# Two cache loads written as eight separate runs per partition, with unpadded source arrays

## The reference

```python
xn = rmsnorm(x, norm1)
z  = xn @ w_in                         # one projection, split into ten parts
a_o, state = hgrn2_scan(...)           # group A: gated linear recurrence, 4 heads of 128
# group B: 8 query heads, 2 key/value heads of 64, keys chosen by an indexer
k_all  = concat([cache_k, b_k])        # 256 cached positions + 16 new ones
ik_all = concat([cache_kidx, i_k])
score  = sum_h w[h] * relu(iq[h] . ik_all)
b_o    = softmax over the top-k keys of q . k_all, times v_all
h = x + concat(a_out, b_o) @ w_o
# PEER: per token 8 heads x 16 experts out of 16384, chosen by product keys
q  = rmsnorm(h) @ wq;  s = q . subkeys;  top 16 of 16 x 16 sums
y  = h + sum over 128 chosen experts of gate * gelu(xn . u[e]) * v[e]
```

## Time and profile before

| what | value |
|---|---|
| median of 3 runs | 1212.73 us (1211.73 to 1213.68) |
| the profiled execution's own time | 1211.73 us |
| its span | 1209.9 us |
| PE busy | 1036.9 us (86%) |
| DVE busy | 807.4 us (67%) |
| ACT busy | 504.7 us (42%) |
| POOL busy | 455.0 us (38%) |
| DMA, mean over the span | 387 GB/s |
| packets of POOL's queue q0 | 55296, 402.68 MB, 82.0% of 16 engines' time |
| packets of SP's queue q1 | 13184, 64.84 MB, 13.3% of 16 engines' time |

### The profile page before, as it was taken

The page is one execution under the profiler, slowest core; times in us unless marked ns, Lnnn a source line. Parts: engine busy times, 40 slices in busy tenths (PEclk is TensorE's granted clock), DMA queues, the critical chain, the costliest instruction groups (busy, mean ns, idle before and its releaser), DMA issues.

```text
span 1209.9 us, 11548 instructions
## 1 busy us (share of the span) xinstructions
PE 1036.9 (86%) x3275; PEld 514.4 (43%) x3275; DVE 807.4 (67%) x1961; ACT 504.7 (42%) x1477; POOL 455.0 (38%) x445
## 2 busy tenths in 40 slices
PE   8997998879789989968888997999986878788786
PEld 4766443544356535524333553455532223222222
DVE  2636666679858476596898647567777567756754
ACT  2535333464554334545436533345333333333333
POOL 0004343443333333443443442443543444444431
PEclk9999999999999999999988998999999999999999
DMA  9957899998798999998999999999999999999997
GB/s 373 410 216 310 299 410 422 397 393 321 312 396 327 380 386 419 414 370 332 422 385 390 410 419 423 417 420 394 398 423 422 422 421 421 421 422 420 422 421 299
DMA packets 68544, 468.25 MB, mean 387 GB/s; under 512 B 7928, under 2 KB 8960, under 8 KB 16896
## 3 DMA queue, kind: packets, MB, share of 16 engines
q0 software_dynamic: 55296, 402.68, 82.0%
q1 hardware_dynamic: 13184, 64.84, 13.3%
HBM read 462.99 MB, written 4.42 MB: 386 GB/s over the span
## 4 chain that ended last, share of the span: by engine, by line
PE 18%; DMA 18%; DVE 9%; ACT 3%; issue 2%; DVEq 0%; ACTq 0%
DMA UV<-in_p_uv,EIDX 17%; PE PSUM L1958 14%; DVE UV L1468 3%; PE PSUM L1737 1%; PE PSUM L1711 1%; DMA WR<-in_st 1%; ACT DIAG L993 1%; DVE EIGHTH L1468 1%; DVE SEL L207 1%; DVE UV L209 1%; ACT WGT L985 1%; DVE SEL L213 1%; DVE SEL L205 0%; DVE SEL L211 0%; ACT GELU L982 0%
## 5 line engine op out<-in xcount | busy, mean ns | idle before, releaser
L1958 PE MATMUL PSUM<-UV,DIAG 128*128 128x512 f32 x1272 | 624.2, 622 | 113.6 <-ACT DIAG L993 112.8
L1468 DVE CUSTOM_DVE_ANT_0 UV<-UV,PSUM 128x1024 f32<-128x1024 f32 x336 | 404.6, 1219 | 212.7 <-DMA UV<-in_p_uv,EIDX 208.9
L566 POOL DMA_INDIRECT UV<-in_p_uv,EIDX x336 | 324.8, 967 | 513.1 <-PE PSUM L1958 467.1
L1958 PEld LDWEIGHTS PSUM<-UV,DIAG 128*128 128x128 f32 x1272 | 231.3, 194 | 436.5 <-ACT DIAG L993 235.3
L982 ACT ACTIVATE GELU<-DOTS 128x1 f32<-128x1 f32 x384 | 77.2, 201 | 444.0 <-DVE DOTS L1468 441.2
L993 ACT ACTIVATE DIAG<-CST,WGT 128x128 f32<-128x128 f32 x366 | 147.0, 402 | 12.0
L1958 PE MATMUL PSUM<-EIGHTH,DIAG 128*128 128x512 f32 x192 | 98.6, 638 | 41.8 <-ACT DIAG L993 41.7
L566 POOL DMA_INDIRECT EIGHTH<-in_p_uv,EIDX x48 | 45.5, 949 | 217.4 <-PE PSUM L1958 115.9
L985 ACT ACTIVATE WGT<-GELU,GATE 128x1 f32<-128x1 f32 x384 | 113.2, 295 | 15.3 <-DVE GATE L1304 2.9
L1958 PEld LDWEIGHTS PSUM<-EIGHTH,DIAG 128*128 128x128 f32 x192 | 35.3, 198 | 92.6 <-ACT DIAG L993 55.4
L1468 DVE CUSTOM_DVE_ANT_0 EIGHTH<-EIGHTH,PSUM 128x1024 f32<-128x1024 f32 x48 | 58.2, 1213 | 23.5 <-DMA EIGHTH<-in_p_uv,EIDX 23.1
(11 more groups left out here) (296 smaller groups left out, 946.2 us busy)
## 6 DMA issues: line engine op xcount, KB each, us to landing
WR<-in_w_o SPq DMA_DIRECT2D x13, 512.0 KB, 11.4
UV<-in_p_uv,EIDX POOLq DMA_INDIRECT x336, 12.0
WR<-in_p_wq SPq DMA_DIRECT2D x10, 512.0 KB, 14.0
UV<-in_w_o SPq DMA_DIRECT2D x2, 2048.0 KB, 14.5
UV<-in_p_wq SPq DMA_DIRECT2D x2, 2048.0 KB, 9.6
WR<-in_w_B SPq DMA_DIRECT2D x2, 2048.0 KB, 8.7
UV<-in_w_B SPq DMA_DIRECT2D x4, 512.0 KB, 7.2
UV<-in_w_B SPq DMA_DIRECT2D x2, 1024.0 KB, 11.6
```

What stands on the lines that cost most here:

```text
L566: nc.gpsimd.indirect_dma_start(ROWS[place_of(n)], None, a["p_uv"], bass.IndirectOffsetOnAxis(EIDX[:, n:n + 1], 0)).then_inc(row_got[place_ ...
L1468: v.tensor_tensor_reduce(out=row, in0=row, in1=XNP, scale=1.0, scalar=0.0, op0=ALU.mult, op1=ALU.add, accum_out=DOTS[:, n % NW:n % NW + 1] ...
L1958: ins = mm(bank[6 + k][:, :], DIAG[:, m % ND, :], VROW[place_of(n)][:, k * 512:(k + 1) * 512], start=n == 0, stop=ends)
```

## The change

The two loads name only the 256 cached positions of each stream as their destination, and the arrays that they read from no longer hold 16 unused positions behind each stream. Before, both sides of the load were one contiguous run of 2176 numbers (8704 bytes) in each partition. Now the source is 2048 contiguous numbers for each partition, and the destination is eight runs of 256 numbers (1024 bytes) with a step of 272 numbers. The last 16 positions of each stream are written by ACT before and after the change.

```diff
@@ -514,12 +514,12 @@
             sp.wait_ge(mixa_ready, 2)
             take(sp, ("ke", 1))
-            sp.dma_start(KTS.rearrange("p b s -> p (b s)"), a["kt"]).then_inc(kts_in, 16)
+            sp.dma_start(KTS[:, :, 0:PAST], a["kt"].rearrange("p (b s) -> p b s", b=BD_)).then_inc(kts_in, 16)
             for k in range(12, 14):
                 load_small(k)
             stored(sp, ("u", 1))
             sp.dma_start(a["ns_p"], ENDS.rearrange("p h n -> p (h n)")).then_inc(st_out, 16)
-            sp.dma_start(IKTS.rearrange("p b s -> p (b s)"), a["ikt"]).then_inc(ikts_in, 16)
+            sp.dma_start(IKTS[:, :, 0:PAST], a["ikt"].rearrange("p (b s) -> p b s", b=BD_)).then_inc(ikts_in, 16)
             for k in range(14, 16):
                 load_small(k)
             take(sp, ("qq", 1, 6))
@@ -2004,10 +2004,8 @@
-
-    room = ((0, 0), (0, 0), (0, TS))
-    o["kt"] = np.pad(i["cache_k"][0].transpose(2, 3, 0, 1).reshape(P, BD_, PAST), room).reshape(P, BD_ * KS)
-    ikt = np.pad(i["cache_kidx"][0].transpose(2, 0, 1), room).reshape(HD, BD_ * KS)
+    o["kt"] = i["cache_k"][0].transpose(2, 3, 0, 1).reshape(P, BD_ * PAST)
+    ikt = i["cache_kidx"][0].transpose(2, 0, 1).reshape(HD, BD_ * PAST)
     o["ikt"] = np.concatenate([ikt, ikt])
```

## The result

The changed kernel took 1227.88 us as a median of 4 runs (1225.39 to 1234.05), the kernel before 1213.20 us beside it (1211.73 to 1216.59): a ratio of 1.0125 with a 95% interval of 1.0082 to 1.0168. It is slower by about 15 us (10 to 20 by the interval), above the forecast of 1218.4 us and outside its range. The profiled execution took 1229.14 us.

The account below looks back on a forecast made before the run. Two DMA queues filling 95% of the engines' time were taken as the bound. Waits of 3.6 and 8.4 us put PE 12.0 us behind, 5.7 passing on: 1211.73 + 5.7 = 1217.4, as a median 1218.4 us; range 1211.8 to 1225.0.

Parts of the forecast that it names:

- Bytes and packet time: Both loads on the DMA engines: 0.3 us less transfer, 1.2 us more piece time, alone costing between nothing and 1.2 us.
- Turns: Two queues sharing a DMA engine alternate piece by piece: 64 turns of 0.36 us, 23.0 us per load against 5.1; chance 0.50.
- rival 2: Turns hold within a gather, but 8 more short pieces pass at each boundary; PE loses 8.5 us, end 1214.9 us; chance 0.17.
- Rival 1: Several short pieces pass in one turn, load stays at about 8 turns; only 1.2 us left, say 1213.0 us; chance 0.22.
- Head 1: PE's query of head 1: weights behind the cached keys land at 475.0, wanted at 471.37, a wait of 3.6 us.
- Head 3: PE's query of head 3: weights behind the indexer keys land at 492.7, wanted at 484.3, a wait of 8.4 us.
- PE's wait of 2.10 us: PE's wait for a late gather, forecast to go because gathers pass faster beside short pieces; counted at nothing.
- What is given back: At DVE's bound stretch, 514 to 550 us: earlier gather landing and PE's 11.2 us of waits cut 12.0 us to 5.7.
- Rival 4: All 12.0 us of PE's delay stay because the later stretch hangs on PE: 1224.7 us; chance 0.05.

## Why the prediction was wrong

- Bytes and packet time: too small to be seen, as said. With both loads later the ratio is 0.9996.
- Turns: right for the time, not for all 16 engines. The keys were forecast to land after about 31 us and took 29.5. What passed in the meantime was not one for one on average. From 448 to 455 us:

```profile
DMA packets 842, 2.87 MB, mean 411 GB/s; under 512 B 47, under 2 KB 546, under 8 KB 561
q0 software_dynamic: 315, 2.30, 80.0%
```

  There are 546 - 47 = 499 short pieces beside 315 packets of q0, 1.6 to one, so some passed in bursts, as rival 2 had it. The last pieces still came at the time of strict turns. In the kernel with only the keys changed, where every piece of 1024 bytes in this place is the keys', the trace's packet records have the first start at 449.9 us and the last at 471.6; 833 of the 1024 had started by 460, and the load landed at 472.5. So a load lands with its slowest engine's last piece, and the 21.7 us from first to last are about the 23.0 of 64 strict turns. The forecast counted every engine as slow; that at least one would get next to no burst was not foreseen. Why some engines got bursts stays open.
- Rival 1, with only 1.2 us and about 8 turns, is refuted by the landing and the waits. Its source, the rule of the Trainium skill in "DMA: Bandwidth & Descriptors", section "Queues, rings and completion order", that an engine drains a packet of typically 9 to 17 descriptors before it switches, is not refuted by the landing alone. By it 64 pieces are 4 to 7 turns, but the prediction let a turn of the gathers be one piece. If the eight pieces that an engine has of a gather pass together as well, 4 to 7 turns are an estimated 13 to 21 us, and the keys would land after 22 to 29.
- The packet records of the trace settle it. Where one piece follows another on an engine, it begins there 2 to 5 ns before the other's end. In the changed kernel from 448 to 460 us, behind 478 gather pieces, a piece of SP's queue begins at that distance 532 times (125 by chance, as counted at other distances), another gather piece 75 times (76 by chance). So a gather piece was not followed by another one: for the gathers the rule does not hold here. Behind SP's pieces another one of SP's begins 695 times (339 by chance) in that stretch, which are the bursts, and 41 times (49 by chance) from 462 to 470 us, where all alternates piece by piece.
- Head 1: forecast 3.6 us, measured 2.1. Head 3: forecast 8.4, measured 8.2. PE's wait of 2.10 us ahead of them was forecast to go, at no gain; it stayed, also in both kernels with the loads later, so it was not the loads beside the gathers that made it.
- **The step that failed is "What is given back".** It took PE's 12.0 us down to 5.7, because the gather of the earlier trace rows would land sooner in an empty queue. The gathers did find one (the DMA share is 0.51 from 490 to 500 us), but DVE's dots of them were not what opened its stretch. Between the dot at 508.06 and L1040 DVE was idle for 4.96 us, waiting for ACT behind PE. That row of before lay six us further on in the same view as the earlier trace rows. PE's 11.2 us of waits are real, but the diagonals of ACT that PE waits for there come from DVE's dots, and DVE's start was late by the same 17.06 us (531.30 against 514.24); they are no slack.
- A term was missing: PE at half clock after each wait, 4.6 us in all by the trace (1.8 behind head 1, 2.8 behind head 3).

The sum with what was measured: 10.3 us of waits, 4.6 us of clock and nothing back make 14.9; the stretch to L1040 grew by 15.2, and the ratio gives 15.2 us. Rival 4, in which all stays, had the right mechanism and only 0.05, and its 12.0 us were still 2.9 short of these 14.9: the clock is missing in it, and its waits are 1.7 us too long.

## What to carry to other kernels

When a load is cut into more pieces, count the pieces in front of whatever stands behind it in the same queue, each at one turn with the other queue's piece, since the slowest engine sets the landing, and put such a load last if its user is far away. Before counting a delay as given back, follow the chain into the next bound stretch from its first instruction backwards; a row shortly before that instruction is not its releaser. Waits of the delayed engine inside that stretch are slack only if the engine that it waits for is not delayed itself.

## What the runs showed of the hardware

- Idle waits of PE for weights of 5.15 to 11.08 us, in seven kernels, were followed by a query of 3.6 to 3.8 us in place of 1.95 and a row of 1.9 to 3.1 in place of 1.88, with a granted clock of 0.52 from 490 to 500 us in the changed kernel. They cost 1.9 to 3.1 us beyond their length, and the longest not the most (2.7). Waits of 2.12 to 2.46 us cost about 1.9 beyond their length, waits of 1.44 and 1.52 about 0.4.
- The length of the wait alone does not tell: the same 2.10 us ahead of head 0's query were followed by a row of 2.82 and a query of 2.82 us in the kernel before, and by 1.98 and 1.95 us in the one before with both loads later.
- With a load of 1024 short pieces ahead in the queue the issue of the next transfers on SP itself became slow: 2.51 and 2.52 us for L521 and L522 (L522 took 0.43 before). With four pieces for each partition, 512 in all, it was 0.43 and 0.57. With only the keys changed it was 2.44 and 2.46, though L522 had its old form there, so it is the pieces ahead that count. SP computes nothing here; what that costs on an engine that does, no run shows.
- Pieces of 2176 bytes, a quarter of the gather's 8192, already moved a load of 1088 KB from 13.7 to 20.5 us beside gathers.
